# Hybrid encoder layer: sums of squares between matmuls, and a first load in halves

## The reference, cut to what matters

```python
xn = rmsnorm(x, g_mix)
u_lru, y_lru, q, k, v, gates = jnp.split(xn @ w_in, IN_SPLITS, axis=-1)
...
q = rmsnorm(q.reshape(B, T, N_HEADS, HEAD_DIM), g_q)
k = rmsnorm(k.reshape(B, T, N_KV_HEADS, HEAD_DIM), g_k)
br_attn = attn_fn(q, k, v, sink) @ w_br_attn
x = x + (g[:, :, 0] * br_lru + g[:, :, 1] * br_attn) @ w_out
...
x = x + (jax.nn.gelu(gc) * up) @ w_down
```

## Time and profile before

| | us |
|---|---|
| median of 3 runs | 1806.59 |
| lowest and highest of them | 1802.4, 1808.53 |
| the profiled execution | 1809.89 |
| its span | 1808.1 |
| TensorE busy in the span | 1794.6 (99%) |
| VectorE, ScalarE, GpSimd busy | 838.0, 561.4, 499.8 |
| mean granted clock of TensorE | 0.992 |

### The profile page before, as it was taken

One profiled execution on the slowest core, in us unless ns is written; L12 is line 12 of the kernel. 1 busy time (PEld: TensorE's weight loads), 2 busy tenths in 40 slices (PEclk: granted clock), 3 DMA queues, 4 the chain that ended last, 5 costly groups with the idle time before them and its releaser, 6 DMA issues.

```text
span 1808.1 us, 29895 instructions
## 1 busy us (share of the span) xinstructions
PE 1794.6 (99%) x11252; PEld 1746.7 (97%) x11252; DVE 838.0 (46%) x1624; ACT 561.4 (31%) x1117; POOL 499.8 (28%) x282
## 2 busy tenths in 40 slices
PE   9999999999999999999999999999999999999999
PEld 8998888899999999999999999999999999999999
DVE  7946757711247676112465555411555511555511
ACT  5535544400156765112133332200322300333300
POOL 3112101122332232333332333332223333333222
PEclk9989989999999999999999999999999999999999
DMA  4011000011111111111311111111111111111113
GB/s 162 25 30 42 24 24 24 24 50 46 39 47 41 52 38 38 47 46 46 143 47 36 46 46 46 47 46 47 46 46 42 41 46 46 46 46 46 46 46 121
DMA packets 28514, 89.16 MB, mean 49 GB/s; under 512 B 3472, under 2 KB 8496, under 8 KB 28464
## 3 DMA queue, kind: packets, MB, share of 16 engines
q1 hardware_dynamic: 25200, 82.49, 13.7%
q10 hardware_dynamic: 3264, 5.96, 1.0%
HBM read 83.70 MB, written 4.73 MB: 49 GB/s over the span
## 4 chain that ended last, share of the span: by engine, by line
PE 95%; DVE 2%; ACT 2%; issue 0%; DMA 0%; SPq 0%; ACTq 0%; DVEq 0%
PE banks L440 85%; PE banks L560 2%; PE banks L575 2%; PE banks L516 1%; PE banks L549 1%; PE banks L526 1%; PE banks L716 1%; PE banks L715 1%; DVE x_lo L1198 1%; DMA resid<-xT 0%; DVE x_lo L1183 0%; DVE resid L1191 0%; ACT prB L910 0%; DVE merged L1206 0%; DVE prB L1298 0%
## 5 line engine op out<-in xcount | busy, mean ns | idle before, releaser
L440 PE MATMUL banks<-x_hi,w_hi 128*128 128x352 f32 x1752 | 578.5, 330 | 4.6 <-DVE x_lo L1183 3.1
L440 PE MATMUL banks<-x_hi,w_lo 128*128 128x352 f32 x1752 | 568.5, 324 | 0.0
L440 PE MATMUL banks<-x_lo,w_hi 128*128 128x352 f32 x1752 | 566.8, 324 | 0.0
L409 POOL TENSOR_SCALAR w_hi<-w_raw 128x1024 fp32r<-128x1024 f32 x137 | 157.0, 1146 | 1238.4 <-DMA w_raw<-W 1238.4
L440 PE MATMUL banks<-h_hi,w_lo 128*128 128x352 f32 x1152 | 372.7, 323 | 0.0
L440 PE MATMUL banks<-h_hi,w_hi 128*128 128x352 f32 x1152 | 372.4, 323 | 0.0
L440 PE MATMUL banks<-h_lo,w_hi 128*128 128x352 f32 x1152 | 371.6, 323 | 0.0
L440 PEld LDWEIGHTS banks<-x_hi,w_hi 128*128 128x128 f32 x1752 | 331.6, 189 | 9.0 <-issue 3.1
L411 POOL TENSOR_TENSOR w_lo<-w_raw,w_hi 128x1024 fp32r<-128x1024 f32 x137 | 334.1, 2439 | 11.4
L440 PEld LDWEIGHTS banks<-x_lo,w_hi 128*128 128x128 f32 x1752 | 331.1, 189 | 2.9
L440 PEld LDWEIGHTS banks<-x_hi,w_lo 128*128 128x128 f32 x1752 | 330.5, 189 | 0.0
(11 more groups left out here) (212 smaller groups left out, 1819.7 us busy)
## 6 DMA issues: line engine op xcount, KB each, us to landing
w_raw<-W SPq DMA_DIRECT2D x139, 512.0 KB, 3.4
resid<-xT SPq DMA_DIRECT2D x6, 704.0 KB, 9.8
sqsum<-xT ACTq DMA_DIRECT2D x2, 2112.0 KB, 13.4
o_yT<-resid SPq DMA_DIRECT2D x8, 528.0 KB, 4.6
wabs<-wab ACTq DMA_DIRECT2D x8, 128.0 KB, 2.0
w_early<-W SPq DMA_DIRECT2D x1, 512.0 KB, 3.7
mat<-mats SPq DMA_DIRECT2D x1, 192.0 KB, 10.1
vec<-vecs SPq DMA_DIRECT2D x1, 143.0 KB, 2.3
```

The lines of the kernel that those rows point to most:

```text
L409: nc.gpsimd.tensor_scalar(w_hi[s][:, :], w_raw[s][:, :], 1.0, 0.0, ALU.mult, ALU.add).then_inc(w_hi_done, 1)
L440: last = nc.tensor.matmul(out[:, 0:cn], w[s if wt is None else wt][:, k * P:(k + 1) * P], x[:, k, cc:cc + cn], start=(k == 0 and j == 0), ...
```

## The change

- **Beginning.** `vec` goes through ScalarE's queue, ahead of its other work. SP issues the left half of slot 0, two rows of x, the right half of slot 0, three more pairs of rows, the two halves of slot 1 and then the rest as before. ScalarE and VectorE split both slots, in halves; GpSimd has nothing to do there. The squares of chunk 0 come behind all of this, on ScalarE. TensorE multiplies zeros four times, not six, and waits for each half of a slot by itself.
- **Keys.** Four of the `key_sum` stand later: (0, 2) by 12 matmuls, (1, 0) by 24, (1, 1) by 12, and (1, 2) goes into the values, behind `v_half(1, 0)`.
- **Sums of the queries.** The 33 sums of half 0 are spread over the 24 k steps of `v_half(0..2, 1)` and `v_half(6..8, 0)`, one or two before each three matmuls; those of half 1 over the last 5 of the 7 k steps of the blocks 12, 13 and 14, two or three each. `v_out(6)` on ScalarE goes ahead of the first exponentials.
- **G0.** `lru_gates(7, 0)` goes two k steps into tile y, `(7, 1)` to step 6 and `(7, 2)` to step 2 of the second chunk. The first branch tile runs k = 0..6 of all three chunks first, and then k = 7 of each.
- **End.** The last row is stored in three chunks.

```diff
@@ -260,0 +261,3 @@
+        s_half, s_w1 = [sem(f"first_half_loaded{s}") for s in range(2)], sem("second_weights_hi")
+        w_first = sem("first_halves_ready")
+        s_x0 = [sem(f"x_rows_loaded{i}") for i in range(KT // 2)]
@@ -330 +333,2 @@
-        SUMS_AT = {NB - 4: range(0, 6), NB - 3: range(6, 12), NB - 2: range(12, NB)}
+        UNITS, SUMS_STEPS = 2 * NC + 1, 24
+        SUMS_BLOCKS, SUMS_FROM = (NB - 5, NB - 4, NB - 3), 2
@@ -367,3 +371,10 @@
-            sp.dma_start(vec[:, :], vecs).then_inc(s_vec, 16)
-            sp.dma_start(w_raw[0][:, :], W[0]).then_inc(wx_loaded, 16)
-            for n, (c0, cn) in enumerate(CHUNKS):
+            left, right = slice(0, DM // 2), slice(DM // 2, DM)
+            sp.dma_start(w_raw[0][:, left], W[0][:, left]).then_inc(s_half[0], 16)
+            for r in range(KT // 2):
+                kk, (c0, cn) = slice(2 * r, 2 * r + 2), CHUNKS[0]
+                sp.dma_start(resid[:, kk, c0:c0 + cn], xT[kk, :, c0:c0 + cn].rearrange("k p n -> p k n")).then_inc(s_x0[r], 16)
+                if r == 0:
+                    sp.dma_start(w_raw[0][:, right], W[0][:, right]).then_inc(wx_loaded, 16)
+            sp.dma_start(w_raw[1][:, left], W[1][:, left]).then_inc(s_half[1], 16)
+            sp.dma_start(w_raw[1][:, right], W[1][:, right]).then_inc(wy_loaded, 16)
+            for n, (c0, cn) in list(enumerate(CHUNKS))[1:]:
@@ -373,2 +383,0 @@
-                    if (n, h) == (0, 0):
-                        sp.dma_start(w_raw[1][:, :], W[1]).then_inc(wy_loaded, 16)
@@ -394 +403 @@
-            for k in range(KT):
+            for k in range(KT - 1):
@@ -397 +406,4 @@
-            sp.wait_ge(s_out, 16 * (6 + 3 + KT))
+            for n, (c0, cn) in enumerate(CHUNKS):
+                sp.wait_ge(y_dve, Y_END - 2 + n)
+                sp.dma_start(yT[KT - 1, :, c0:c0 + cn], resid[:, KT - 1, c0:c0 + cn]).then_inc(s_out, 16)
+            sp.wait_ge(s_out, 16 * (6 + 3 + KT + 2))
@@ -414,2 +426 @@
-            pool.sem_inc(w_hi_done, 1)
-            split(0, (1,))
+            pool.sem_inc(w_hi_done, 2)
@@ -461 +472 @@
-            def last_row(sem_, value):
+            def last_row(sem_, value, chunk_=None):
@@ -466 +477 @@
-                return before
+                return before if chunk_ is None else lambda k: before(chunk_, k)
@@ -489,0 +501,4 @@
+                    if n == 0 and k == 0:
+                        pe.wait_ge(w_first, s + 1)
+                    elif n == 0 and k == KT // 2:
+                        pe.wait_ge(wx_ready if s == 0 else wy_ready, 1)
@@ -497 +512 @@
-            for _ in range(6):
+            for _ in range(4):
@@ -510 +525 @@
-            def v_half(tt, s):
+            def v_half(tt, s, sums=None):
@@ -514,0 +530,2 @@
+                    if sums is not None:
+                        query_sums(0, sums + k - 4 * s, SUMS_STEPS)
@@ -520 +537 @@
-            def query_sums(a, b):
+            def query_sums(a, step, steps):
@@ -522,2 +539,2 @@
-                for u in range(units_of(b)):
-                    t0 = SMP if b == NC else b * CHUNK + u * DSEQ
+                for i in range(step * UNITS // steps, (step + 1) * UNITS // steps):
+                    t0 = SMP if i == UNITS - 1 else i * DSEQ
@@ -525 +542 @@
-                    at = SUMS_COL[a] + 2 * (2 * b + u)
+                    at = SUMS_COL[a] + 2 * i
@@ -527,2 +544,2 @@
-                if b == NC:
-                    last.then_inc(a_qs, 1)
+                    if i == UNITS - 1:
+                        last.then_inc(a_qs, 1)
@@ -579 +596 @@
-            def beside(s, p, n, ks):
+            def beside(s, p, n, ks, before=None):
@@ -590 +607 @@
-                chunk(s, n, x_hi, x_lo, to=n, ks=ks)
+                chunk(s, n, x_hi, x_lo, before, to=n, ks=ks)
@@ -592,2 +609,3 @@
-            def fill(work):
-                for (s, p, n), ks in work:
+            def fill(g):
+                for (s, p, n), ks in fill_of(g):
@@ -596 +614,18 @@
-            pe.wait_ge(wx_ready, 1)
+            def fill_with_sums(g):
+                at, steps = 0, sum(len(ks) for _, ks in fill_of(g)) - SUMS_FROM
+                first = steps * SUMS_BLOCKS.index(g)
+                def before(k):
+                    nonlocal at
+                    if at == SUMS_FROM:
+                        pe.wait_ge(a_lo, g)
+                        if g == SUMS_BLOCKS[0]:
+                            pe.wait_ge(x_act, out_before(PAIR_G))
+                            pe.wait_ge(y_act, out_before(PAIR_G))
+                    if at >= SUMS_FROM:
+                        query_sums(1, first + at - SUMS_FROM, steps * len(SUMS_BLOCKS))
+                    at += 1
+                for (s, p, n), ks in fill_of(g):
+                    beside(s, p, n, ks, before)
@@ -598 +632,0 @@
-            pe.wait_ge(wy_ready, 1)
@@ -623 +657 @@
-                elif (n, k) == (1, 0):
+                elif (n, k) == (1, 4):
@@ -625 +658,0 @@
-                    key_sum(1, 0)
@@ -626,0 +660,2 @@
+                    key_sum(1, 0)
+                elif (n, k) == (2, 4):
@@ -636 +670,0 @@
-            key_sum(1, 2)
@@ -641,0 +676,2 @@
+                if tt == 1:
+                    key_sum(1, 2)
@@ -642,0 +679,2 @@
+            pe.wait_ge(h_sqd, 12)
+            pe.wait_ge(h_rt, 5)
@@ -644 +682 @@
-                v_half(tt, 1).then_inc(v_done, 1)
+                v_half(tt, 1, 4 * tt).then_inc(v_done, 1)
@@ -648,5 +686 @@
-                v_half(tt, 0).then_inc(x_done, 1)
-                if tt == 6:
-                    pe.wait_ge(h_sqd, 12)
-                for b in SUMS_AT[tt - 6 + NB - 4]:
-                    query_sums(0, b)
+                v_half(tt, 0, 4 * (tt - 3)).then_inc(x_done, 1)
@@ -666 +700,2 @@
-            fill(fill_of(0)[1:])
+            for (s, p, n), ks in fill_of(0)[1:]:
+                beside(s, p, n, ks)
@@ -672,5 +706,0 @@
-                if g in SUMS_AT:
-                    pe.wait_ge(x_act, out_before(PAIR_G))
-                    pe.wait_ge(y_act, out_before(PAIR_G))
-                    for b in SUMS_AT[g]:
-                        query_sums(1, b)
@@ -679 +709,4 @@
-                fill(fill_of(g))
+                if g in SUMS_BLOCKS:
+                    fill_with_sums(g)
+                else:
+                    fill(g)
@@ -691 +724,9 @@
-            def gated(p0, stage, between=None, second=None, before=None):
+            def last_gates(n, k):
+                if (n, k) == (0, 2):
+                    pe.wait_ge(s_wab, 16 * KT)
+                    lru_gates(KT - 1, 0)
+                elif (n, k) in ((0, 6), (1, 2)):
+                    lru_gates(KT - 1, n + 1)
+            def gated(p0, stage):
@@ -696,3 +737 @@
-                if between is not None:
-                    between()
-                tile(1, 0, p0, x_hi, x_lo, y_act, ya, before=second)
+                tile(1, 0, p0, x_hi, x_lo, y_act, ya, before=last_gates)
@@ -700,3 +739,6 @@
-                if before is not None:
-                    pe.wait_ge(r_lo, START + 3 * (KT - 1))
-                tile(0, 0, p0 + 1, c_hi, d_lo, before=before)
+                pe.wait_ge(r_lo, START + 3 * (KT - 1))
+                pe.wait_ge(wx_ready, p0 + 2)
+                for n in range(3):
+                    chunk(0, n, c_hi, d_lo, ks=range(KT - 1))
+                for n in range(3):
+                    chunk(0, n, c_hi, d_lo, last_row(r_lo, START + 3 * (KT - 1), n), ks=range(KT - 1, KT))
@@ -726,10 +768 @@
-            def gates_first():
-                pe.wait_ge(s_wab, 16 * KT)
-                lru_gates(KT - 1, 0)
-            def gates_later(n, k):
-                if (n, k) in ((0, KT // 2), (1, 0)):
-                    lru_gates(KT - 1, n + 1)
-            gated(PAIR_G0, "G0", gates_first, gates_later, last_row(r_lo, START + 3 * (KT - 1)))
+            gated(PAIR_G0, "G0")
@@ -830,0 +864 @@
+            act.dma_start(vec[:, :], vecs).then_inc(s_vec, 16)
@@ -834,2 +868,3 @@
-            act.wait_ge(wx_loaded, 16)
-            A(w_hi[0][:, :], w_raw[0][:, :], ACT.Copy).then_inc(s_w0, 1)
+            left, right = slice(0, DM // 2), slice(DM // 2, DM)
+            act.wait_ge(s_half[0], 16)
+            A(w_hi[0][:, left], w_raw[0][:, left], ACT.Copy).then_inc(s_w0, 1)
@@ -837,3 +872,13 @@
-            for h in range(2):
-                unscaled_hi(0, h)
-                squares(0, (h,))
+            for r in range(KT // 2):
+                c0, cn = CHUNKS[0]
+                act.wait_ge(s_x0[r], 16)
+                for k in (2 * r, 2 * r + 1):
+                    A(x_hi[:, k, c0:c0 + cn], resid[:, k, c0:c0 + cn], ACT.Copy, scale=V("g_mix", k)).then_inc(x_rhi, 1)
+                if r == 1:
+                    act.wait_ge(wx_loaded, 16)
+                    A(w_hi[0][:, right], w_raw[0][:, right], ACT.Copy).then_inc(s_w0, 1)
+            act.wait_ge(s_half[1], 16)
+            A(w_hi[1][:, left], w_raw[1][:, left], ACT.Copy).then_inc(s_w1, 1)
+            act.wait_ge(wy_loaded, 16)
```

(18 more changed lines are left out.)

2 lines of the change are left out of this document (1 added, 1 removed).

## The result

The changed kernel takes **1793.5 us** (median of four executions, 1793.23 to 1796.04), the kernel before, beside it on the same chip, 1807.56 us: a ratio of **0.9929**, 95% interval 0.9904 to 0.9953. The forecast was 1795.0 us. The profiled execution is one of 1793.23 us, with a span of 1791.5 us, 16.6 us shorter than the 1808.1 of before.

What follows compares the result with a forecast made beforehand. TensorE, 99% busy, was taken as the bound, with waits and half-clock stretches. Terms 3.0 + 0.5 + 6.0 + 1.4 + 3.4 - 0.2 + 0.8 = 14.9 us off the profiled 1809.9 gave 1795.0 us; range 1789 to 1808.

Steps and rivals of the forecast that it cites:

- The clock: TensorE: spread sums keep the granted clock at 1.00, returning 7.8 us in half 0 and 4.7 in half 1, before exits.
- rival 1: Spread sums: the clock still falls within half 0's steps or half 1's blocks; 1800 to 1808 us, likeliest 1804; chance 0.27.
- Rival 3: Sums are not the cause, idleness alone lowers the clock: 2.4 us gained, 1807.5 us; chance 0.03.
- Rival 2: Half 0's 24 steps: the mixture holds the clock down, 32.8 us instead of 17.7; total about 1813 us; chance 0.10.
- Sums of half 0: Spreading the first half's query sums: 7.8 us of clock back, less 1.8 for exits, 6.0 us gained.
- Half 1: Spreading the second half's sums in attention blocks: 4.7 us of clock back less 15 exits of 0.085, 3.4 us gained.
- `v_out(6)`: Moved ahead of the first exponentials on ScalarE: TensorE's wait for it goes, 1.4 us gained.
- The beginning: Start up to norm_sums(0): smaller, earlier loads and no GpSimd subtraction beside x_lo, 3.0 us gained, between 1.5 and 4.5.
- What follows, up to the keys: Between the beginning and the keys: matmuls and norm form a chain that moves as one with the beginning's gain.
- Keys: Later key sums remove a 1.5 us wait for a root, 1.1 returns at the query tile's copy; 0.5 us gained.
- G0: Two waits of 0.9 and 0.5 us go, but tile y waits for the gate; 0.2 us lost.
- End: The last store carries 176 KB instead of 528: 0.8 us gained, between 0.3 and 1.2.

Runs made afterwards that it cites:

- a_grouped: The changed kernel with the query sums put back into three groups per half at the old places: 1803.18 us, ratio 0.9979 to the kernel before.
- b_spread: The kernel before with only its sums spread as in the change: 1798.98 us, ratio 0.9954 to the kernel before.
- a_dense: The changed kernel with half 0's sums in 12 steps instead of 24: 1801.3 us, ratio 0.9967 to the kernel before.
- a_wide: The changed kernel with sums grouped again, each sum row multiplying by 128 columns instead of 2: 1797.93 us, ratio 0.9947 to the kernel before.
- a_squares: The changed kernel with x_sums(0, 1) behind the x_lo of chunk 2, norm_sums(0) and norm_spread(0) later: 1796.65 us.
- a_g0_rows: The changed kernel with the branch tile's k = 7 rows of chunks 0 and 1 earlier: 1793.58 us, ratio 0.9919 to the kernel before.
- a_again: The changed kernel once more, unaltered, on another chip: 1795.76 us, ratio 0.993 to the kernel before.
- a_quarters: The changed kernel with every 128x1024 instruction of GpSimd's weight splits cut into four of 128x256: 1794.17 us, ratio 0.992 to the kernel before.
- a_pool: The changed kernel with GpSimd's split of w_early moved behind its splits of pair 1: 1795.7 us.

## Why the prediction was right

The time and its main cause came as forecast: 1793.5 and 1795.8 measured, 1795.0 predicted, with a clock of 1.00 throughout. Not every term did, and errors of both signs partly cancel: the two halves of the sums and `v_out(6)` gave 3.9 us more than forecast in the trace, the wait for `dg` and G0 took 1.9 back. So the closeness of 1795.0 is in part luck. To take the total of the profiled execution for the new median, though that execution is 3.3 us over the old one, was sound: the spread of the kernel before is in the main the clock (1801.5 us at a mean of 0.997, 1807.7 to 1810.9 at 0.990 to 0.992), and the change takes that away.

- **The clock: right, and shown to be the cause.** Grouping the sums brings 0.50 back (a_grouped), spreading them alone removes it (b_spread). Rivals 1 and 2 didn't come; at twice the density rival 1 does (a_dense). Rival 3 is refuted for the four stretches at the sums: TensorE is busy throughout them, and they go with the groups. The first stretch (14.14 to 17.55) is another matter. There, in a_wide, b_spread and a_squares the fall stands behind or among waits, and no run here removes a wait alone to prove it. The Trainium skill, TensorE: Matmul & The Clock Gate, What's actually happening, says that activity releases the lower clock and that an idle stretch brings it back. The stretches among waits agree with it, though not every wait had one behind it. At the sums TensorE had a matmul in flight for all of 5.00 us at 0.50 (a_grouped), and was at 1.00 in the same place with 128 columns a row (a_wide), so being occupied was not enough.
- **Rival 2's own sum** is slightly off: 138 rows and matmuls at 0.21 and 24 exits of 0.14 are 32.3 us, not 32.8. It changes nothing.
- **Sums of half 0: 6.0 forecast, 7.8 found** (from the first matmul of `v_half(3, 0)` to the first scores, 130.18 and 120.51: 9.67, less the 1.87 from ahead of it). **Half 1: 3.4 forecast, 5.2 found**, of which 0.5 is less waiting for the exponentials (1.0 in the trace of before, 0.5 now). The term that was wrong is "it costs exits: the first matmul behind sums comes 0.20 us on, not 0.12". The clock's 7.8 and 4.7 came back whole. I had read the exit at the end of a group, and not that an entry saves as much.
- **`v_out(6)`: 1.4 forecast, 1.7 found** from the first scores to `scores(1)`. The wait is gone; beside spread sums it would have been 2.8 (b_spread). The term was taken at its size before the other edit.
- **The beginning: 3.0 forecast, 2.92 measured**, by the route described: first matmul at 6.55 (6.7), no x_lo over 0.6 us, `norm_sums(0)` at 25.85 (25.8). Within it the second pair of x came late (x_hi at 7.58, forecast 6.9), and the wait for x_lo of chunk 2 was 1.27, not 1.8. That the clock stays at 1.00 here was in part luck: the prediction counts the first stretch at 0.50 among the 4.5 us, reckons with it gone, and never says why it should go. In a_wide and a_g0_rows, with the same beginning, it is there, and `norm_sums(0)` comes at 26.43 and 26.29.
- **"What follows, up to the keys, is a chain of matmuls and norm that moves as one": this failed,** though the total hides it. It moved by 2.9 us on TensorE and by 1.2 on GpSimd, and half of the beginning's gain was given back 5 us later. The earlier trace rows held the hint: x_lo of row 3 took 2.68 us beside GpSimd's subtraction of 2.51. I priced only the removal of that one meeting, and did not ask which others the change would make.
- **Keys: 0.5 forecast, 0.45 measured** (1.42 to 1.87). The new wait is 0.95, forecast 1.1.
- **G0: 0.2 lost forecast, 0.6 measured** (16.49 to 15.90), within the bounds. The two waits come back as 0.5 for the gates (0.1 to 0.5) and 1.8 for the gate's activation (1.5 to 2). The sum had the branch tile start 0.8 earlier, with the wait for the gates at 0.1, the least of its own range; it started 0.5 earlier.
- **End: 0.8 forecast, 0.8 measured.** The last join stands 15.8 us earlier and the span ends 16.6 earlier.

The profiled execution of before, 1809.89 us, is among the longest of its kind (1801.5 to 1810.27 in the runs beside a_grouped). So the 16.6 us between the two traces are more than the gain of the medians, 12 to 14 us; in medians the sums are worth 8.6 us (b_spread) or 7.4 (a_grouped against a_again, on two chips).

## What to carry to other kernels

Read the granted clock by windows beside the busy share: an engine that is busy all through a stretch can run it at half its clock, and groups of matmuls with two columns did that here. Mix them among wide ones and try the density: 24 steps were enough here and 12 were not. When a change moves one engine by a few microseconds, look at which VectorE instructions then stand beside GpSimd's long ones; and when waits that are removed one at a time only move on, try the removals together before giving up. When an edit removes a wait and gains nothing, look at the clock behind the wait that took its place.

## What the runs showed that was not expected

- **GpSimd and VectorE hold each other up for a whole instruction.** Products of 128x6 and 128x4 took 1.66 and 1.96 us instead of 0.15 to 0.17 beside a GpSimd subtraction of 2.4 us, and ended with it; beside quarters, 0.46 and 0.66. A reciprocal and a multiplication that reads PSUM ran through in the same stretch (0.19 and 0.16 us at 26.98 and 27.20). The Trainium skill, SBUF — State Buffer, Who interferes with whom, states it: a VectorE instruction with both inputs in SBUF, or in a two-port mode, and a GpSimd instruction that reads SBUF exclude each other, and the later one waits for the whole of the earlier. The traces agree, in both directions: in a_quarters it is GpSimd's subtraction that is held up, 4.19 us instead of 2.8.
- **When weights land decides what the hold strikes.** A shift of 0.6 us in GpSimd's start went with 2.1 us more waiting in the attention (2.6 against 0.5), between two executions of the same kernel. Whether this makes up all of the 2.9 us between executions stays open, since a_quarters has as much.
- **The lower clock came with rows of two columns and not with rows of 128**, at the same places in the program: 10.2 us at 0.50 in half 0 against none.
- **The lower clock also came beside waits of TensorE, with no group of sums near**: 3.4 to 6.8 us at 0.50 around and behind a wait of 1.9 for x_lo (before, b_spread) and of 2.2 for nacc (a_squares), at a cost larger than the wait in a_squares. Waits of 1.4 us for `dg` or 2.3 at norm_spread(1) (a_pool) had no such stretch behind them, so a wait of that length does not do it every time.
